# The gated-linear-attention projection in another order: k first, the gate's 16 columns beside half of q, and a shorter gate chain

## The reference

```python
def odd_mixer(h, w_in, w_gate, b_gate, norm_g, w_out):
    proj = h @ w_in
    q, k, v, r, g_lr = jnp.split(
        proj, [GLA_KEY, 2 * GLA_KEY, 2 * GLA_KEY + GLA_VAL, 2 * GLA_KEY + 2 * GLA_VAL], axis=-1)
    g = jax.nn.log_sigmoid((g_lr @ w_gate + b_gate).astype(jnp.float32)) / GATE_TAU
    ...
    o = gla_chunked(qh, kh, vh, gh)
    o = merge_heads(rms_norm(o, norm_g)).astype(h.dtype)
    return (o * jax.nn.silu(r)) @ w_out
```

## Time and profile before

| | |
|---|---|
| median of three runs (lowest, highest) | 1518.47 us (1518.05, 1519.51) |
| time of the profiled execution | 1518.41 us |
| its span in the profile | 1516.6 us |
| TensorE busy | 1459.8 us, 96% of the span |
| VectorE, ScalarE, GpSimd busy | 952.1, 716.8, 159.3 us |
| chain that ended last, TensorE's share | 42% |

### The profile page before, as it was taken

How to read it: one execution, slowest core, us unless ns; L and a number is a source line. 1 busy time by engine, 2 the same in 40 slices (tenths; PEclk the granted TensorE clock), 3 DMA queues, 4 the chain that set the end, 5 groups by cost and what they waited for, 6 DMA issues and landing times.

```text
span 1516.6 us, 17986 instructions
## 1 busy us (share of the span) xinstructions
PE 1459.8 (96%) x6819; PEld 1201.7 (79%) x6819; DVE 952.1 (63%) x1314; ACT 716.8 (47%) x1034; POOL 159.3 (11%) x260
## 2 busy tenths in 40 slices
PE   7999999999999999999989999999999999799997
PEld 6888878778888788887768788887877788688886
DVE  5666567777666576665577766655568566665553
ACT  5544355455444354443464454443556644254441
POOL 0800010000000000000053100000543110000000
PEclk9999999999999999999989999999999999899999
DMA  8766745147666667664623486653645354365551
GB/s 265 258 201 223 252 137 193 36 139 261 211 202 249 201 224 235 207 229 141 202 94 118 146 263 202 220 190 132 209 139 193 127 168 166 111 211 178 176 199 55
DMA packets 200661, 279.15 MB, mean 184 GB/s; under 512 B 8772, under 2 KB 124016, under 8 KB 200576
## 3 DMA queue, kind: packets, MB, share of 16 engines
q1 hardware_dynamic: 200320, 277.90, 55.1%
q10 hardware_dynamic: 256, 0.11, 0.0%
HBM read 276.93 MB, written 1.05 MB: 183 GB/s over the span
## 4 chain that ended last, share of the span: by engine, by line
PE 42%; issue 4%; DVE 3%; ACT 1%; POOL 1%; DVEq 0%; POOLq 0%; ACTq 0%
PE ps L527 13%; PE ps L530 13%; PE ps L528 13%; PE ps L1319 1%; PE ps L800 1%; DVE xtmp L1624 1%; ACT junk L631 1%; DVE wlo L448 0%; PE ps L689 0%; ACT xh L718 0%; POOL st L640 0%; DVE ps L1704 0%; PE ps L1811 0%; DVE ps L1572 0%; PE ps L1685 0%
## 5 line engine op out<-in xcount | busy, mean ns | idle before, releaser
L448 DVE TENSOR_TENSOR wlo<-raw,whi 128x1024 fp32r<-128x1024 f32 (+2 forms) x474 | 564.8, 1222 | 211.1 <-ACT whi L439 210.7
L527 PE MATMUL ps<-whi,xh 128*128 128x512 f32 (+2 forms) x1440 | 575.7, 400 | 19.2 <-ACT xh L718 12.7
L528 PE MATMUL ps<-wlo,xh 128*128 128x512 f32 (+2 forms) x1440 | 562.1, 390 | 0.0
L530 PE MATMUL ps<-whi,xl 128*128 128x512 f32 (+2 forms) x1440 | 554.4, 391 | 0.8 <-DVE xl L713 0.7
L439 ACT ACTIVATE whi<-raw 128x1024 fp32r<-128x1024 f32 (+2 forms) x474 | 469.5, 1043 | 165.0 <-PE ps L530 154.5
L527 PEld LDWEIGHTS ps<-whi,xh 128*128 128x128 f32 x1440 | 274.7, 191 | 77.4 <-issue 18.7
L530 PEld LDWEIGHTS ps<-whi,xl 128*128 128x128 f32 x1440 | 274.0, 190 | 58.7 <-DVE xl L713 1.7
L528 PEld LDWEIGHTS ps<-wlo,xh 128*128 128x128 f32 x1440 | 274.8, 191 | 52.3 <-issue 0.2
L527 PE MATMUL ps<-whi,gh 128*128 128x512 f32 x440 | 173.1, 393 | 0.0
L528 PE MATMUL ps<-wlo,gh 128*128 128x512 f32 x440 | 171.5, 390 | 0.0
L530 PE MATMUL ps<-whi,gl 128*128 128x512 f32 x440 | 153.6, 390 | 0.0
(11 more groups left out here) (244 smaller groups left out, 967.8 us busy)
## 6 DMA issues: line engine op xcount, KB each, us to landing
raw<-in_ffn_w_in_dram SPq DMA_DIRECT2D x174, 512.0 KB, 5.1
raw<-in_ffn_w_out_dram SPq DMA_DIRECT2D x40, 1024.0 KB, 5.1
raw<-in_w_in_dram SPq DMA_DIRECT2D x26, 1024.0 KB, 5.0
adat<-in_w_ada_dram SPq DMA_DIRECT2D x96, 256.0 KB, 5.4
raw<-in_gla_w_in_dram SPq DMA_DIRECT2D x12, 1024.0 KB, 5.2
raw<-in_w_ffn_gate_dram SPq DMA_DIRECT2D x22, 512.0 KB, 4.0
raw<-in_w_ffn_up_dram SPq DMA_DIRECT2D x22, 512.0 KB, 5.1
raw<-in_hyb_w_in_dram SPq DMA_DIRECT2D x10, 1024.0 KB, 5.1
```

The source lines that it names most:

```text
L448: e.tensor_tensor(split_of(wlo, j), raw_of(j), split_of(whi, j).bitcast(F32), ALU.subtract).then_inc(*wlo_made.up(j))
L527: e.matmul(ps[:, 0:n], a, whi_of(j, k), start=first and k == 0, stop=False)
L528: last = e.matmul(ps[:, 0:n], a, wlo_of(j, k), start=False, stop=False)
L530: last = e.matmul(ps[:, 0:n], b, whi_of(j, k), start=False, stop=final and k == subs[j][2] - 1)
```

## The change

The chunks are now k; the upper half of q's columns (256 to 511) with the 16 gate columns beside them in one chunk of 272; the lower half of q; then v and r as before. k's transposes stand at i = 3 of c1; the transposes of the gate columns at i = 1 of c2, the gate products and the gate chain at i = 3 of c2; q's transposes ahead of c3, where k's stood. Right behind the copy that ends the gate columns' transposition, ScalarE loads one table set that has both Exp and Ln. In the chain, ScalarE takes the absolute value with the bias straight from PSUM, then Exp and Ln per half; VectorE adds the bias and takes the minimum straight from PSUM (per head), and the scans subtract as they add, so that the separate subtraction is gone. The steps of levels 1 to 8 stand where they stood.

```diff
-        GLA_COLS = ((0, 512), (3072, 16), (512, 512), (1024, 512), (1536, 512), (2048, 512), (2560, 512))
+
+        GLA_COLS = (((512, 512),), ((256, 256), (3072, 16)), ((0, 256),), ((1024, 512),), ((1536, 512),), ((2048, 512),),
+                    ((2560, 512),))
...
-        for c, n in GLA_COLS:
-            plan_cols(T["gla_w_in"][0], c, n, 8)
+        for parts in GLA_COLS:
+            plan_parts([(T["gla_w_in"][0], c, n) for c, n in parts], 8)
...
-        GLA = ["keys", None, None, (0, 0), (0, 1), None, None, None]
+        GLA = ["q", None, None, (0, 0), (0, 1), None, None, None]
...
-            if s == "keys":
-                pe_turn(e, ("gk",), hid[1], [gla_in.at(2, 0), gla_in.at(2, 1)], gla_turned, gla_qk)
+            if s == "q":
+                pe_turn(e, ("gq",), hid[0], [gla_in.at(2, 0), gla_in.at(2, 1)], gla_turned, gla_qk)
...
-                e.wait_ge(*gla_qk.at("gk", 2 * j))
+                e.wait_ge(*gla_qk.at("gq", 2 * j))
...
-            def turn_q(i):
+            def turn_k(i):
+                if i == 3:
+                    pe_turn(e, ("gk",), hid[1], [gla_in.at(0, 0), gla_in.at(0, 1)], gla_turned, gla_qk)
+
+            def turn_low(i):
                 if i == 1:
-                    pe_turn(e, ("gq",), hid[0], [gla_in.at(0, 0), gla_in.at(0, 1)], gla_turned, gla_qk)
-
-            def turn_low(i):
-                if i == 3:
                     ps = tb.next(("lr",), (lr_made,))
                     for done in tb.freed:
                         e.wait_ge(*done)
                     for tok in range(2):
-                        e.wait_ge(*gla_in.at(1, tok))
+                        e.wait_ge(*gla_in.at("lr", tok))
                         t = e.transpose(ps[0:16, tok * P:(tok + 1) * P], lr[:, tok * 16:tok * 16 + 16], ident)
                     t.then_inc(*lr_turned.up())
-            pe_chunk(e, 4, GJ[1], [(gla_in, 1, tok) for tok in range(2)], turn_q)
+                if i == 3:
+                    for hp in range(2):
+                        pe_gate_dot(e, hp)
+            pe_chunk(e, 4, GJ[1], [(gla_in, "lr", tok) for tok in range(2)], turn_k)
             pe_chunk(e, 4, GJ[2], [(gla_in, 2, tok) for tok in range(2)], turn_low)
             for c in range(3, 7):
                 def at(i, c=c):
-                    if c == 3 and i == 1:
-                        for hp in range(2):
-                            pe_gate_dot(e, hp)
                     for s in gla_steps(4 * (c - 3) + i):
                         pe_gla_step(e, s)
                 pe_chunk(e, 4, GJ[c], [(gla_in, c, tok) for tok in range(2)], at)
...
-            ps = tb.next(("gate", hp), (gate_biased, 2 * hp + 1))
+            ps = tb.next(("gate", hp), (gate_min, 2 * hp + 1))
...
-                if c == 1:
-                    dst, src, f = lr[:, tok * 16:tok * 16 + 16], ps[:, 0:16], ACT.Copy
-                elif c < 3:
-                    dst, src, f = hid[0 if c == 0 else 1][:, o], ps[:, :], ACT.Copy
+                if c < 3:
+                    q = {0: o, 1: slice(tok * 512 + 256, tok * 512 + 512), 2: slice(tok * 512, tok * 512 + 256)}[c]
+                    dst, src, f = hid[0 if c else 1][:, q], ps[:, 0:256 if c else 512], ACT.Copy
                 else:
                     z, k = (gv, c - 3) if c < 5 else (gr, c - 5)
                     dst, src = z[:, tok * D + k * 512:tok * D + (k + 1) * 512], ps[:, :]
                     f = ACT.Copy if c < 5 else ACT.Silu
                 e.activation(dst, src, f, scale=rstd(("h", 4, tok))).then_inc(*gla_in.up(c, tok))
+                if c == 1:
+                    e.activation(lr[:, tok * 16:tok * 16 + 16], ps[:, 256:272], ACT.Copy, scale=rstd(("h", 4, tok))
+                                 ).then_inc(*gla_in.up("lr", tok))
 
             act_open(e, 4, before, lambda tok: evac(0, tok))
             for c in range(1, 7):
                 for i in range(4):
                     act_begin(e, GJ[c] + i)
-                    if c == 2 and i == 3:
+                    if c == 2 and i == 1:
                         e.wait_ge(*lr_turned.at())
                         e.activation(lrT[:, :], tb.of("lr")[0:16, 0:256], ACT.Copy).then_inc(*lr_made.up())
-                    if c == 3 and i == 1:
+                        e.preload_act_table_set("natural_log_exp_and_others")
+                    if c == 2 and i == 3:
                         act_gates(e)
                     if c >= 3:
                         for s in gla_steps(4 * (c - 3) + i):
...
         def act_gates(e):
+
             E1 = gX[0]
             for hp in range(2):
                 e.wait_ge(*gate_dot.at(hp))
                 for j in range(2):
                     hd = 2 * hp + j
                     e.activation(E1[:, hd * 256:(hd + 1) * 256], tb.of("gate", hp)[:, j * 256:(j + 1) * 256],
-                                 ACT.Identity, bias=vector("bg", hd)).then_inc(*gate_biased.up(hd))
+                                 ACT.Abs, bias=vector("bg", hd)).then_inc(*gate_abs.up(hd))
                 x = slice(hp * 512, (hp + 1) * 512)
-                e.wait_ge(*gate_min.at(hp))
-                e.activation(E1[:, x], E1[:, x], ACT.Abs).then_inc(*gate_abs.up(hp))
-            e.wait_ge(*gate_abs.at(1))
-            e.activation(E1[:, :], E1[:, :], ACT.Exp, scale=-1.0).then_inc(*gate_exp.up())
-            e.wait_ge(*gate_exp.at())
-            e.activation(E1[:, :], E1[:, :], ACT.Ln, bias=1.0).then_inc(*gate_ln.up())
+                e.wait_ge(*gate_abs.at(2 * hp + 1))
+                e.activation(E1[:, x], E1[:, x], ACT.Exp, scale=-1.0).then_inc(*gate_exp.up(hp))
+                e.wait_ge(*gate_exp.at(hp))
+                e.activation(E1[:, x], E1[:, x], ACT.Ln, bias=1.0).then_inc(*gate_ln.up(hp))
         def dve_gates(e):
+
+            E1, G = gX[:2]
             for hp in range(2):
-                x = slice(hp * 512, (hp + 1) * 512)
-                e.wait_ge(*gate_biased.at(2 * hp + 1))
-                e.tensor_scalar(gX[1][:, x], gX[0][:, x], 0.0, None, ALU.min).then_inc(*gate_min.up(hp))
-
-        def dve_decays(e):
-            E1, G = gX[:2]
-            e.wait_ge(*gate_ln.at())
-            e.wait_ge(*gate_min.at(1))
-            e.tensor_tensor(G[:, :], G[:, :], E1[:, :], ALU.subtract).then_inc(*gate_log.up())
-            e.wait_ge(*gate_log.at())
-            for j in range(8):
-                y = slice(j * P, (j + 1) * P)
-                e.tensor_tensor_scan(gB[:, y], ones[:, :], G[:, y], 0.0, ALU.mult, ALU.add
-                                     ).then_inc(*decay_made.up(j))
+                e.wait_ge(*gate_abs.at(2 * hp + 1))
+                for j in range(2):
+                    hd = 2 * hp + j
+                    e.tensor_scalar(G[:, hd * 256:(hd + 1) * 256], tb.of("gate", hp)[:, j * 256:(j + 1) * 256],
+                                    vector("bg", hd), 0.0, ALU.add, ALU.min).then_inc(*gate_min.up(hd))
+            for hp in range(2):
+                e.wait_ge(*gate_ln.at(hp))
+                e.wait_ge(*gate_min.at(2 * hp + 1))
+                for j in range(4 * hp, 4 * hp + 4):
+                    y = slice(j * P, (j + 1) * P)
+                    e.tensor_tensor_scan(gB[:, y], G[:, y], E1[:, y], 0.0, ALU.add, ALU.subtract
+                                         ).then_inc(*decay_made.up(j))
         def dve_gla(e):
             j0 = J0[4]
             for c in range(1, 7):
                 for i in range(4):
                     dve_begin(e, GJ[c] + i)
-                    if c == 1 and i == 1:
+                    if c == 1 and i == 3:
                         for b0 in (0, 2):
-                            e.wait_ge(*gla_turned.at("gq", b0))
-                            e.tensor_scalar(by_4(gQT)[:, b0:b0 + 2, :], turned(("gq",), b0), P ** -0.5, None, ALU.mult
-                                            ).then_inc(*gla_qk.up("gq", b0))
-                    if c == 3 and i == 1:
+                            e.wait_ge(*gla_turned.at("gk", b0))
+                            e.tensor_scalar(by_4(gKT)[:, b0:b0 + 2, :], turned(("gk",), b0), 1.0, None, ALU.mult
+                                            ).then_inc(*gla_qk.up("gk", b0))
+                    if c == 2 and i == 3:
                         dve_gates(e)
```

## The result

| | before | changed |
|---|---|---|
| median of four runs (lowest, highest) | 1518.68 us (1518.05, 1519.51) | 1508.00 us (1505.48, 1508.24) |
| profiled execution, its span | 1518.41 us, 1516.6 us | 1505.48 us, 1503.7 us |

The forecast of 1506.3 lies between the changed kernel's profiled execution and its median.

The account below looks back on a forecast made before the run. TensorE, busy for 96% of the span, was taken to bound the kernel. Terms -3.9 - 2.4 - 4.8 - 1.0 = -12.1 us took 1518.4 to 1506.3 us, range 1501.5 to 1511.5.

Parts of the forecast that it names:

- What bounds: Whole kernel: TensorE is busy for 96% of the span, so only less TensorE work, shorter waits or kept clock count.
- Narrow matmuls and clock in c1 and c2, -8.0: Chunks c1 and c2: 4.6 us less from replacing 16-column matmuls, 3.4 us less from full instead of half clock.
- the rival of half clock for 264 columns: c1 and c2: 264-column matmuls beside transposes and gate products fall to half clock, +11.6 us, gain 0.5; chance 0.06.
- c2 ends at 743.4: End of c2 on TensorE: 728.80 + 11.6 matmuls + 1.0 transposes + 2.05 gate products = 743.4.
- The wait for q: Ahead of c3: TensorE waits some 3 us for c2's evacuation behind ScalarE's gate chain; q's transposes start 746.5, 3.9 us earlier.
- From there to c4: q's transposes to c4: 16.0 us in place of 18.4, including 2.0 for half clock; c4 starts at 762.5.
- The level-1 wait: TensorE ahead of the level-1 scores: waits 2.2 us (0.7 to 3.5) in place of 7.05, 4.8 less.
- S: Start of c3's last evacuation, from which level 1 was timed: products end at S+7.6, TensorE comes at S+5.4.
- Half clock behind it, "every second time", 0.9: Behind the level-1 wait: half clock cost 1.9 us before, now comes every second time, 0.9; 1.0 us less.
- the sum's 3.9, 2.4, 4.8 and 1.0: Forecast gains in us: q's transposes earlier, from there to c4, level-1 wait, clock behind it; together 12.1.
- One for one afterwards: Behind level 1: steps stand as before relative to c4 to c6, TensorE nearly always busy, so the lead is kept.
- The slower rival: Gate chain: if c3's second-half unit came late, TensorE would wait one for one; decides from a 23 us landing; chance 0.04.

Follow-up runs that it names:

- second profile: The changed kernel run once more with nothing edited, against a kernel before of 1518.32 us: 1506.88 us, ratio 0.9921.

## Why the prediction was right, step by step

- **What bounds**: right. TensorE's share stayed at 96% while work, clock and waits left it together.
- **Narrow matmuls and clock in c1 and c2, -8.0**: right, in kind and size. The columns alone brought 8.0 us up to the transposes ahead of c3, 0.2 of it a shorter wait; 7.5 in the stage and 6.5 in the median are what is left once the long level-1 wait and its clock have taken their part. The clock of c1 and c2 is 1.00 in every profile, so the rival of half clock for 264 columns falls.
- **c2 ends at 743.4**: its last matmul starts at 743.83, 0.12 apart from the others, so 743.95 less 0.25, 743.7.
- **The wait for q**: 3.07 us for 3.0, the transposes at 746.9 for 746.5. ScalarE's queue was placed row by row, and it came out to 0.3 us (the evacuation ends at 747.04, less 0.25, for 746.5). The biased pair was 0.82, Exp and Ln 0.64 and 0.63, for 0.84, 0.63 and 0.63 in the sum.
- **From there to c4**: c3's last evacuation starts at 762.3 for 762.5, after 1.7 us lost to half clock (0.57 over 4 us), for 2.0. The sum had taken this half clock to follow short pauses too, as in the kernel before (0.83 in c3, with pauses of 0.87 and 0.69). That doesn't hold in general: with the old chain and the new columns the same place has pauses of 0.66 and 0.69 and a clock of 1.00.
- **The level-1 wait**: 2.06 us for 2.2; from S (762.59) to the end of it 7.45 us for 7.6, with one product at 2.01 beside GpSimd. The mechanism is as described; that the sum hit it to 0.15 is partly luck, since 7.6 was picked between 6.1 and 8.9.
- **Half clock behind it, "every second time", 0.9**: as a mean that was good, since half clock stands behind such a wait in two of five profiles. For one execution it is 0 or 1.7. In the first profile it is 0, and that is the larger part of the 1.3 us between the predicted 12.1 and the stage's 13.4. Term by term the sum's 3.9, 2.4, 4.8 and 1.0 came to 3.5, 3.1, 5.0 and 1.8, so smaller misses on either side went into one another. In the second profile, with its 1.7, the stage is 12.0 us shorter. The medians, with gains of 10.7 and 11.4, stand below the forecast. The sum held none of what varies outside the stage, up to 2.5 us at one place; how much of it is in the medians is open.
- **One for one afterwards**: nearly. 13.4 us of the stage became 12.9 of the span.
- **The slower rival**: in the profile no wait of TensorE, ScalarE or SyncE in the stage ended with a transfer; it did not happen. That it would decide from 23 us was not tried.

One sentence that the sum did not need but the reading suggests would have been wrong: that the early place of the gates ends the long level-1 wait. The short chain with one load ends it, from either place. How the 5.9 us of the short chain divide between the loads, the direct reads of PSUM and the scans that no longer stand behind two splits was not measured apart; of the loads it is only known that without the one ahead of the chain some 6 to 7 us are lost at the new place.

## What to carry to other kernels

Place the queue of the engine that a wait hangs on row by row, each at the duration of its nearest row; that gave four points in time within 0.4 us. When a chain is moved earlier, look at what now stands behind it on its engine (here an evacuation, then PSUM copies): the move alone was worth nothing that could be measured, and the order behind it was worth 3 to 5 us. And price a TensorE wait at its length plus a chance of clock: here waits of 0.66 us ahead of c3 had none behind them (four profiles), those of 2.06 to 2.41 had 1.7 us or nothing (two of five), and those of 3.05 to 3.07 had 1.4 to 1.7 each time (three).

## What the runs showed of the hardware

- The same TensorE wait, 2.06 us long in two executions of one kernel, was followed by half clock (0.77, 0.50, 0.87 over 6 us) in one and by full clock in the other; the same happened from 1050 us on, where it cost 2.5 us by 1297.
- TensorE was at 0.87 and 0.82 over 48 matmuls of 16 columns and what followed them, though busy for 20.77 of the 20.8 us, and at 1.00 over 96 of 272 and 256 columns in every profile here. The clock fell at 734, near the end of the narrow ones. The new order also moved the transposes beside them, and no run has the one without the other.
- A table load costs 1.28 us, and the activation behind it starts within 0.02 us of its end, four times in one chain and once at level 1.
- A product of two SBUF tiles on VectorE took 2.01 us beside a GpSimd product and 0.68 behind it. VectorE's reads of PSUM of 256 columns with a bias from a column took 0.44 us each (0.87 and 0.88 for two), as ScalarE's evacuations of the same width did (0.47).
